# Retention's values a dense step later, two norms' turns shifted, and two weight splits held back in a two-block float32 transformer kernel

## What is computed

```
# first block; h = rmsnorm(x) * (1 + scale1) + shift1
qa, ka, va, iq, ik, iw, qr, kr, vr, gr, ga, gb = split(h @ w_in)
y_a = topk_attention(qa, ka, va, iq, ik, iw) @ w_attn_proj
# retention: 4 heads, chunks of 128 rows, keys 128 wide, values 256 wide
inner = (q_n @ k_n.T) * dmask                 # chunk n, head h
o     = inner @ v_n + (q_n @ state) * qdec    # "values"
state = state * cdec + (k_n * kdec).T @ v_n   # "update"
y_r = (silu(gr) * head_groupnorm(o)) @ w_ret_proj
x = x + gate1 * ((sigmoid(ga) * y_a + sigmoid(gb) * y_r) @ w_out)        # wo0, wo1
h2 = rmsnorm(x) * (1 + scale2) + shift2                                  # norm "n2"
x = x + gate2 * ((silu(h2 @ w_gate) * (h2 @ w_up)) @ w_down)             # up, dn
x = rmsnorm(x)                                                           # last norm
# second block
z = rms_norm(x) @ w_in_2                                                 # norm "n3"; 2kv, 2kw, 2nq, ...
x = x + concat(nsa_mixer(z), gla_mixer(z)) @ w_out_2                     # 2wn, 2wg
u = causal_conv3(rms_norm(x) @ w_up_2)                                   # norm "n4"; 2up
out = x + (silu(u_gate) * u_up) @ w_down_2                               # 2dn
```

## Time and profile before

| | us |
|---|---|
| median of 3 runs | 1574.42 (1573.48 to 1574.72) |
| the profiled execution | 1571.98 |
| its span in the trace | 1570.2 |
| PE busy | 1546.0 (98%), 7987 instructions |
| PEld busy | 1249.6 (80%) |
| DVE busy | 871.5 (56%) |
| ACT busy | 607.0 (39%) |
| POOL busy | 44.2 (3%) |

### The profile page before, as it was taken

How to read it: one execution, slowest core, us unless ns; L and a number is a source line. 1 busy time by engine, 2 the same in 40 slices (tenths; PEclk the granted TensorE clock), 3 DMA queues, 4 the chain that set the end, 5 groups by cost and what they waited for, 6 DMA issues and landing times.

```text
span 1570.2 us, 19653 instructions
## 1 busy us (share of the span) xinstructions
PE 1546.0 (98%) x7987; PEld 1249.6 (80%) x7987; DVE 871.5 (56%) x1581; ACT 607.0 (39%) x1038; POOL 44.2 (3%) x82
## 2 busy tenths in 40 slices
PE   7999999999999999999999999999999999999999
PEld 5777888788888888888888886776778888888887
DVE  6679785665365753322243575786466545655432
ACT  4453334542322532222233354665425433344330
POOL 0000000000000000000000011100010000000000
PEclk9999999999999999999999999999999999999999
DMA  9323122146344244222322133110113233222311
GB/s 386 130 79 106 44 79 68 55 147 238 112 160 162 95 173 161 94 94 82 107 98 103 41 111 135 54 44 12 55 59 129 81 108 107 94 89 86 120 68 54
DMA packets 44882, 165.75 MB, mean 106 GB/s; under 512 B 5108, under 2 KB 5236, under 8 KB 43640
## 3 DMA queue, kind: packets, MB, share of 16 engines
q1 hardware_dynamic: 44792, 164.50, 30.1%
HBM read 162.38 MB, written 2.10 MB: 105 GB/s over the span
## 4 chain that ended last, share of the span: by engine, by line
PE 92%; DVE 5%; ACT 1%; issue 1%; POOL 0%; DMA 0%; SPq 0%; DVEq 0%; ACTq 0%
PE bank L548 88%; PE bank L557 4%; DVE wl L1725 1%; DVE AR L1737 1%; DVE X L1737 1%; DVE Hl L1737 0%; DVE G L1744 0%; ACT wh L1207 0%; POOL ST L2556 0%; DVE CST L1737 0%; DMA CST<-in_cst 0%; ACT AR L1218 0%; DVE AR L2047 0%; DVE AR L1744 0%; DVE AR L1740 0%
## 5 line engine op out<-in xcount | busy, mean ns | idle before, releaser
L1207 ACT ACTIVATE wh<-raw 128x1024 fp32r<-128x1024 f32 (+1 forms) x197 | 205.7, 1048 | 387.7 <-PE bank L548 375.5
L548 PE MATMUL bank<-wh,Hh 128*128 128x512 f32 (+1 forms) x784 | 318.1, 406 | 1.9 <-DVE Hl L1737 1.0
L1725 DVE TENSOR_TENSOR wl<-raw,wh 128x1024 fp32r<-128x1024 f32 (+1 forms) x197 | 236.7, 1209 | 139.4 <-ACT wh L1207 138.6
L548 PE MATMUL bank<-wh,Hl 128*128 128x512 f32 (+1 forms) x784 | 303.6, 387 | 0.0
L548 PE MATMUL bank<-wl,Hh 128*128 128x512 f32 (+1 forms) x784 | 303.1, 387 | 0.0
L548 PE MATMUL bank<-Hh,wh 128*128 128x512 f32 (+2 forms) x712 | 268.6, 377 | 1.1 <-DVE AR L1737 0.7
L548 PE MATMUL bank<-Hl,wh 128*128 128x512 f32 (+2 forms) x712 | 266.9, 375 | 0.0
L548 PE MATMUL bank<-Hh,wl 128*128 128x512 f32 (+2 forms) x712 | 266.9, 375 | 0.0
L548 PEld LDWEIGHTS bank<-wh,Hh 128*128 128x128 f32 x784 | 147.2, 188 | 49.9 <-issue 22.7
L548 PEld LDWEIGHTS bank<-wh,Hl 128*128 128x128 f32 x784 | 147.2, 188 | 31.0
L548 PEld LDWEIGHTS bank<-wl,Hh 128*128 128x128 f32 x784 | 147.5, 188 | 25.4
(11 more groups left out here) (251 smaller groups left out, 1854.4 us busy)
## 6 DMA issues: line engine op xcount, KB each, us to landing
raw<-in_wst SPq DMA_DIRECT2D x268, 512.0 KB, 3.6
AR<-in_wst SPq DMA_DIRECT2D x8, 1024.0 KB, 10.7
X<-in_x SPq DMA_DIRECT2D x8, 512.0 KB, 5.7
AR<-in_wst SPq DMA_DIRECT2D x5, 512.0 KB, 5.6
out<-X SPq DMA_DIRECT2D x8, 256.0 KB, 2.1
CST<-in_cst SPq DMA_DIRECT2D x1, 1619.0 KB, 11.3
raw<-in_wst SPq DMA_DIRECT2D x4, 296.0 KB, 2.8
BC<-in_bc SPq DMA_DIRECT2D x2, 512.0 KB, 9.0
```

The costliest lines, as they stand in the source:

```text
L548: return e.matmul(o, l, r, start=start, stop=stop, skip_group_check=True)
L1207: e.activation(HI[slot[i]][:, 0:width(i)], raw[:, i % NR, 0:width(i)], ACT.Copy).then_inc(*w_hi.mark(i))
L1725: e.tensor_tensor(LO[slot[i]][:, 0:n], raw[:, i % NR, 0:n], HI[slot[i]][:, 0:n].bitcast(f32), SUB).then_inc(*w_lo.mark(i))
```

## The change

Three edits. (1) `schedule`: while ticks of `dn` are planned, the piece ("2kv", 2) may be split only at a tick of the last contraction piece (21), and ("2kv", 3) at none. (2) The turns of n2 and n4 come 5, 5, 4, 3 ticks after their tile's end for tiles 0 to 3, instead of 4 for each; DVE's row scaling comes 3, 3, 3, 2 ticks after it instead of 2, and `norm_low` one after the turn. (3) In retention PE's value block and the DVE block stand three yields behind the scores instead of two, and one trailing yield is gone, so that a pair still takes as many yields as before. No instruction is added or taken away on any engine, and SP's order of DMAs is the same. The merge of the two attention paths is the same in both kernels.

```diff
@@ schedule
             elif at in rank:
                 while avail and avail[0][0] >= NH and not (...):
                     avail.pop(0)
+
+                if name == "dn" and (what[1] < 21 and chunks[at][:2] == ("2kv", 2) or chunks[at][:2] == ("2kv", 3)):
+                    break
                 ahead = 5 if name != "iq" else 3 if what[0] == 7 else what[0] % 2
@@ program
+        TURN = (5, 5, 4, 3)
@@ tensor_program, retention
                         free[4] = dve.of(("inner", t, hp))
                         yield
                         yield
+                        yield
                         on.wait_ge(*dve.of(("inner", t, hp)))
...
                         yield
-                        yield
                         if hp:
                             yield
                             yield
@@ tensor_program, n2 (n4 likewise at 2wg)
-... lambda t: w.after(4, lambda: norm_turn("n2", t)))
+... lambda t: w.after(TURN[t], lambda: norm_turn("n2", t)))
@@ scalar_program, retention
-                        yield
-                        yield
-                        yield
+                        for _ in range(4):
+                            yield
                         on.wait_ge(*dve.of(("normed", t, hp)))
...
-                        yield
                         if hp:
@@ scalar_program, n2 and n4: norm_gain after TURN[t] instead of 4
@@ vector_program, retention: as in tensor_program
@@ vector_program, n2 (n4 likewise)
-                            w.after(2, lambda t=t: norm_scale("n2", t))
-                            w.after(4, lambda t=t: norm_gain("n2", t))
-                            w.after(5, lambda t=t: norm_low("n2", t))
+                            w.after((3, 3, 3, 2)[t], lambda t=t: norm_scale("n2", t))
+                            w.after(TURN[t], lambda t=t: norm_gain("n2", t))
+                            w.after(TURN[t] + 1, lambda t=t: norm_low("n2", t))
```

More of the change, by code:

```diff
@@ L894, in tensor_program @@
             by_tile("wo0", ["wo0"], 8, merged, HM, lambda t, n: dve.of(("wo0", t)))
-            by_tile("wo1", ["wo1"], 8, merged, HM, lambda t, n: dve.of(("wo1", t)), lambda t: w.after(4, lambda: norm_turn("n2", t)))
+            by_tile("wo1", ["wo1"], 8, merged, HM, lambda t, n: dve.of(("wo1", t)), lambda t: w.after(TURN[t], lambda: norm_turn("n2", t)))
             def up(prefix, tag, freed, fourth=None):
@@ L1191, in tensor_program @@
             by_tile("2wg", ["2wg0", "2wg1"], 4, lambda k, t: H(k + 4, t), lambda t: dve.of(("g", "low", t, 0)), lambda t, n: dve.of(("2wg", t, n)),
-                    lambda t: w.after(4, lambda: norm_turn("n4", t)))
+                    lambda t: w.after(TURN[t], lambda: norm_turn("n4", t)))
             up("2up", "n4", lambda j, m: dve.of(("2up", "conv", 2 * j + m if m < 2 else 22 + 2 * j + m - 2)))
@@ L1476, in gain2 @@
                         norm_gain("n2", t, dense.of(("wo1", t, 0)))
-                    w.after(4, gain2)
+                    w.after(TURN[t], gain2)
             def early_halves(of, freed):
@@ L1684, in scalar_program @@
                     norm_root("n4", t, dve.of(("2wg", t, 0)), dve.of(("2wg", t, 1)))
-                    w.after(4, lambda t=t: norm_gain("n4", t, dense.of(("2wg", t, 1))))
+                    w.after(TURN[t], lambda t=t: norm_gain("n4", t, dense.of(("2wg", t, 1))))
             for j, a, c in w.steps("2up"):
@@ L2517, in vector_program @@
                     if n:
-                        w.after(2, lambda t=t: norm_scale("n4", t))
-                        w.after(4, lambda t=t: norm_gain("n4", t))
-                        w.after(5, lambda t=t: norm_low("n4", t))
+                        w.after((3, 3, 3, 2)[t], lambda t=t: norm_scale("n4", t))
+                        w.after(TURN[t], lambda t=t: norm_gain("n4", t))
+                        w.after(TURN[t] + 1, lambda t=t: norm_low("n4", t))
             cw = W("cw").rearrange("p (w c) -> p w c", w=3)
```

## The result

The changed kernel takes 1567.31 us (median of 5 runs, 1564.71 to 1568.16), the kernel before 1574.42 (1572.92 to 1574.79, 5 runs). The ratio is 0.9956, with a 95% interval of 0.9941 to 0.997: 7.1 us less, where the forecast was 5.7. The profiled execution of the changed kernel took 1567.2 us with a span of 1565.4, so the profile shows 4.8 us of the gain.

The account below looks back on a forecast made before the run. PE, busy 1546.0 us of a 1570.2 us span, bounds the kernel, so only its waits can be won. Retention 0.8, n2 1.9, the splits 2.2 and n4 0.8 sum to 5.7 us: 1568.7 us, range 1566.5 to 1571.9.

Parts of the forecast that it names:

- Retention: At retention's value blocks on PE: gain 1.26 less 0.45 of new wait, so 0.8 us, bounds −0.5 to 2.1.
- p3's wait: PE's wait at the value block of pair p3 in retention goes, with 1.1 us to spare: gain 1.26 us.
- p6's: PE's wait of 0.84 us at pair p6's value block in retention stays, held by one line from block to inner product.
- Norm n2: At n2's first two turns, bank 3 and last wait: 0.60 + 0.58 + 0.83 − 0.4 + 0.29 = 1.9 us, bounds 0.6 to 2.55.
- The turn of tile 2: In n2, PE's turn of tile 2 newly waits 0.3 to 0.4 us for a scaling that ends at 542.35.
- The splits: At n3, two DVE splits moved behind dn's last residual and the scaling end PE's wait: 2.2 us, bounds 1.4 to 2.27.
- Norm n4: At n4's bank 3, the residual now stands ahead of a scaling that waits for POOL: 0.8 us, bounds 0 to 1.0.
- all eight waits go: Rival: all eight of PE's waits at the touched places go and none comes: 7.7 us, 1566.7 us; chance 0.15.
- the turns only move the waits: Rival: n2's shifted turns bring new waits that cost the gain, n4 gives nothing: 3.0 us, 1571.4 us; chance 0.15.
- the splits' gain is given back: Rival: PE waits longer at later waits, in the stages after the splits: gain 3.5 us, 1570.9 us; chance 0.08.
- the splits come too late: Rival: at the fifth tick of 2kv PE waits for the held-back splits: slower, above 1574.4 us; chance 0.04.
- nothing changes: Rival: the waits are the profile's and the true time is set elsewhere: within 3 us of before; chance 0.03.

Follow-up runs that it names:

- ret_only: The kernel before with the third edit alone, retention's value blocks a dense step later; 1572.58 us, ratio 0.9995.
- act_later: The changed kernel with ACT's scaling of retention's outputs one yield later, behind the evacuations of the q and k tiles; 1564.72 us, ratio 0.994.
- act_before: The kernel before with ACT's scaling of retention's outputs moved behind the evacuations; 1574.32 us, ratio 1.0.
- hold_only: The kernel before with the two held-back splits of 2kv alone; 1571.32 us, ratio 0.9984.
- late4: The changed kernel with the split of piece 3 of 2kv held back four more ticks, behind n3's gain and Hl on DVE; 1569.81 us, ratio 0.9973.
- The half edits: Two runs of the changed kernel, with DVE's scalings of n2 and n4 put back (1570.2 us) or their turns put back (1571.04 us).
- before_again: The kernel before, unchanged, run once more to see the granted clock in each run; 1573.49 us, ratio 1.0003.
- hold_three: The changed kernel with only one of the two splits held back, piece 3 of 2kv; 1566.59 us, ratio 0.9954.

## Why the prediction was right, and where its sizes were off

**What bounds it.** Right. PE's busy sum moved by 0.7 us, the gain came from its gaps, and at n3 the gap priced by starts (bracket + 0.16) agrees with the stage: 2.27 foreseen, 2.29 measured. Each part alone gave its share. All four terms were too small, by 0.25, 0.44, 0.09 and 0.36, and the sum of 5.7 us was 1.1 too small against 6.84. The 7.1 of the medians is just beyond the 4 to 7 us that I had called the forecast's own range, and inside the bounds.

**Retention.** 0.8 forecast, 1.05 measured (0.93 to 0.95 alone). p3's wait went, p6's stayed (0.71 for 0.68), and p7's came, with a bracket of 0.24, about 0.40 from start to start where I had 0.45. The times that I had worked out for p3 hold on before's clock, 0.95 us less than the rows: the DVE block started at 190.36 (190.5 at most foreseen), the inner product row ended at 194.90 (195.1), and PE's value block started at 196.21 (196.2). That is so although the rope that now stands ahead of the block waited 1.40 us for ACT's evacuation, which I hadn't foreseen. p3's wait was worth 1.36 us in ret_only's starts and not 1.26. That p6 hangs on a line through ACT was right and was shown by act_later; act_before showed that DVE's queue was as long.

**Norm n2.** 1.9 forecast, 2.34 measured. The step that was mis-sized is "The turn of tile 2 ... waits 0.3 to 0.4". It doesn't wait. I let the scaling start 0.3 earlier than in the earlier trace rows, "also held by a split". It started at 541.11, 0.8 earlier (0.1 of that is the offset of the two traces): the residual of tile 2 began at 537.32 instead of 538.31. The split ahead of it, which began at 537.16 after 0.26 us of waiting for ACT, stands in front of the Hl rows now (534.98) and waits for nothing; and the root was ready when DVE came to the scaling. It ended at 541.86 and PE turned at 541.91, so this was close: 0.05 us. And the 0.25 that I left for Hl of tile 3 was nearly right as a loss without a bracket (552.59, 0.36 for 0.12).

**The splits.** 2.2 forecast, 2.29 measured; hold_only gave 2.32. The cover that I gave as 0.9 and 0.8 us (1.0 and 0.8 by my own times) was 1.1 and 0.9. The price past it, about a microsecond for each (3.14 for 2.9), is what late4 shows.

**Norm n4.** 0.8 forecast, 1.16 measured, beyond my upper bound of 1.0. The two gaps that go, 0.82 and the small one of 0.17, carry two more: after each the next start also comes late (0.23 after 1206.58 in the earlier trace rows where 0.12 is usual), together 0.18. The term missed this.

**The rivals.** That all eight waits go (1566.7) is nearer to the measured 1567.31 than my 1568.7 is, but for another reason: p6's stayed and p7's came, and the n2 and n4 terms were larger. That the turns only move the waits, that the splits' gain is given back, that the splits come too late, or that nothing changes, did not happen. The half edits show that the first of these was no idle fear: with one half of the edit it does.

**The clock.** I foresaw nothing here. The times of one kernel spread by 3 to 4 us (before: 1571.76 to 1575.51 in 33 runs), and the mean clock of a run goes with its time: for the changed kernel 1564.71 at 1.000, 1567.31 at 0.999, 1567.2 to 1568.16 at 0.998. The runs of before at 1.000 in the later comparisons took 1571.62 to 1573.08, so 6.9 to 8.4 us more than the one of the changed kernel at 1.000. These runs belong to other comparisons than the changed kernel's, so this is a rough check; it fits the 6.84 of the stages at its lower end.

## What to carry to other kernels

When one engine is busy for 98% and in order, price each of its waits by the starts around it and not by the bracket, and ask for every one which instruction of the other engine stands ahead of the late one without being needed; moving that away won 6.8 us here without any instruction less. A shift of the consumer and a shift of the producer can belong together: here each alone won nothing over the two norms, since a wait came back or grew elsewhere. Before holding work back, read the tick at which it is needed: 1 us of cover was enough here, and beyond it every microsecond cost one.

## What the runs showed of the hardware

TensorE's granted clock falls to 1.2 GHz for some microseconds in part of the executions, and in these profiles only in an idle time of PE or soon behind one. At about 19 us six of the thirteen profiles have a dip, in or behind waits of 1.57 to 1.98 us (before_again: 1.98 us, and a mean of 0.77 over its window of 15 us), and at 1000 us three of thirteen, all after the same wait of 1.79 us. It is not certain after such a wait: late4 and hold_three waited 1.59 and 1.61 us at the first place and kept 1.00, and ten profiles kept it at the second. Waits of 0.99 to 1.30 us at the first place were never followed by one. A dip at 1000 us costs 1.04 to 1.10 us. The start of the kernel takes 64.0 to 65.9 us in the six profiles with a dip at 19 us and 62.6 to 64.0 in the other seven. The Trainium skill, page TensorE: Matmul & The Clock Gate, section What's actually happening, says that the clock's gate is set by how busy TensorE has been lately. The traces agree in that the clock fell only in or soon after idle time. I had not reckoned with it: where two orders differ by one microsecond, these dips hide it from the times, and the starts in the trace show it.

A gap in a stream of 256-column matmuls costs a little more than itself, since the next start is late by 0.07 to 0.11 us as well.
